# The recurrence's projection: order of its column blocks, and where the bonus product is kept

## The reference

```python
proj = h @ w_in
z, q_mem = proj[..., :RW_SHIFT], proj[..., RW_SHIFT:]
z_prev = jnp.pad(z, ((0, 0), (1, 0), (0, 0)))[:, :-1]
z = z + (z_prev - z) * mu
r, k, v, zw, za, zg = _split(z, [MIX_WIDTH] * 3 + [DECAY_LORA, ICLR_LORA, GATE_LORA])
w_log = -jax.nn.softplus(-(w0 + jnp.tanh(zw) @ w2)) - 0.5
decay = jnp.exp(-jnp.exp(w_log.astype(jnp.float32)))
a = jax.nn.sigmoid(a0 + za @ a2)
g = jax.nn.sigmoid(zg) @ g2
kk = (k * k_k).astype(jnp.float32).reshape(B, S, H, N)
kk = kk / jnp.maximum(jnp.sqrt(jnp.sum(kk * kk, axis=-1, keepdims=True)), 1e-12)
k = k * (1 + (a - 1) * k_a)
...
y = _wkv7_scan(rh, wh, kh, vh, -kk, kk * ah)
...
bonus = jnp.sum(rh * kh * r_k.astype(jnp.float32), axis=-1, keepdims=True) * vh
out = (y + bonus.reshape(B, S, MIX_WIDTH)) * g.astype(jnp.float32)
```

## Time and profile before

| what | us |
|---|---|
| median of 3 runs | 2264.17 (2262.78 to 2269.66) |
| the profiled execution, its own time | 2262.99 |
| its span | 2261.1 |
| TensorE busy | 2106.9 (93%) |
| VectorE busy | 1143.5 (51%) |
| ScalarE busy | 826.4 (37%) |
| mean granted TensorE clock | 0.971 |

### The profile page before, as it was taken

The page is one execution under the profiler, slowest core; times in us unless marked ns, Lnnn a source line. Parts: engine busy times, 40 slices in busy tenths (PEclk is TensorE's granted clock), DMA queues, the critical chain, the costliest instruction groups (busy, mean ns, idle before and its releaser), DMA issues.

```text
span 2261.1 us, 36356 instructions
## 1 busy us (share of the span) xinstructions
PE 2106.9 (93%) x15617; PEld 1141.8 (51%) x15617; DVE 1143.5 (51%) x1755; ACT 826.4 (37%) x1344; POOL 274.1 (12%) x342
## 2 busy tenths in 40 slices
PE   6898889999999998799999999998998888999998
PEld 3566554444444343688744444553565435444444
DVE  4865763444432368665545455234637455655221
ACT  4324763232322664332243234323335334332222
POOL 2311331000001010222210000102012113000000
PEclk9998999999999999999999999998999999999999
DMA  6442002433222312000033433241320021323220
GB/s 147 118 142 67 2 1 70 116 95 107 89 96 84 93 54 75 21 22 4 3 93 95 112 93 103 93 140 57 112 75 20 19 75 38 112 93 110 95 93 38
DMA packets 203844, 173.61 MB, mean 77 GB/s; under 512 B 20416, under 2 KB 179332, under 8 KB 203684
## 3 DMA queue, kind: packets, MB, share of 16 engines
q1 hardware_dynamic: 202778, 170.34, 24.9%
q10 hardware_dynamic: 906, 0.96, 0.2%
HBM read 169.18 MB, written 2.10 MB: 76 GB/s over the span
## 4 chain that ended last, share of the span: by engine, by line
PE 79%; DVE 10%; ACT 6%; issue 3%; POOL 1%; ACTq 0%; DMA 0%; DVEq 0%; POOLq 0%
PE banks L1119 46%; PE banks L1162 17%; PE banks L1410 4%; PE banks L1200 1%; DVE w_lo L2227 1%; ACT w_hi L1679 1%; PE banks L1422 1%; POOL arena L969 1%; ACT arena L1784 1%; PE banks L1220 1%; PE banks L1599 1%; PE banks L1177 1%; PE banks L1522 1%; DVE banks L2325 1%; ACT arena L2069 1%
## 5 line engine op out<-in xcount | busy, mean ns | idle before, releaser
L1119 PE MATMUL banks<-arena,w_hi 128*128 128x512 f16 (+1 forms) x2160 | 628.7, 375 | 5.5 <-DVE arena L2247 3.3
L2227 DVE TENSOR_TENSOR w_lo<-wring,w_hi 128x2048 bf16<-128x2048 f32 (+3 forms) x162 | 357.2, 2206 | 473.8 <-ACT w_hi L1679 470.1
L1679 ACT ACTIVATE w_hi<-wring 128x2048 f16<-128x2048 f32 (+3 forms) x162 | 294.9, 1822 | 462.3 <-PE banks L1162 266.1
L1119 PE MATMUL banks<-arena,w_lo 128*128 128x512 f16 (+1 forms) x1080 | 404.4, 374 | 0.0
L1162 PE MATMUL banks<-arena,w_hi 128*128 128x512 f16 x1216 | 363.2, 381 | 10.9 <-DVE xT L2304 4.4
L1119 PEld LDWEIGHTS banks<-arena,w_hi 128*128 128x128 f16 x2160 | 211.2, 98 | 251.8 <-DVE arena L2247 5.7
L1119 PE MATMUL banks<-h_hi,w_hi 128*128 128x512 f16 (+1 forms) x624 | 239.7, 384 | 18.7 <-DVE w_lo L2227 9.6
L969 POOL TENSOR_TENSOR arena<-arena,ntmp 128x512 f32<-128x512 f32 (+1 forms) x79 | 100.9, 1278 | 1262.6 <-ACT ntmp L1709 1257.1
L1119 PE MATMUL banks<-h_lo,w_hi 128*128 128x512 bf16 (+1 forms) x624 | 239.3, 384 | 0.0
L1119 PE MATMUL banks<-h_hi,w_lo 128*128 128x512 f16 (+1 forms) x624 | 238.9, 383 | 0.0
L1162 PE MATMUL banks<-arena,w_lo 128*128 128x512 f16 x608 | 231.3, 380 | 0.0
(11 more groups left out here) (392 smaller groups left out, 2687.9 us busy)
## 6 DMA issues: line engine op xcount, KB each, us to landing
wring<-in_w_ffn_in SPq DMA_DIRECT2D x88, 512.0 KB, 5.0
wring<-in_w_ff SPq DMA_DIRECT2D x32, 1024.0 KB, 5.1
wring<-in_w_ffn_out SPq DMA_DIRECT2D x20, 1024.0 KB, 5.1
wring<-in_rw_w_in SPq DMA_DIRECT2D x11, 1024.0 KB, 5.2
wring<-in_w_in SPq DMA_DIRECT2D x11, 1024.0 KB, 5.2
wring<-in_nsa_w_in SPq DMA_DIRECT2D x7, 1024.0 KB, 5.3
wring<-in_w_mem_kv SPq DMA_DIRECT2D x4, 1024.0 KB, 5.1
wring<-in_w_o SPq DMA_DIRECT2D x4, 1024.0 KB, 5.1
```

What stands on the lines that cost most here:

```text
L1119: last = mm(v, p[0], p[1], start=(i == 0), stop=(i == len(prods) - 1))
L1679: A(w_hi[:, at[0] % NSPLIT, 0:w["size"]], wring[:, w["slot"], 0:w["size"]], ACT.Copy).then_inc(split_hi, 1)
L2227: V.tensor_tensor(w_lo[:, sl, 0:w["size"]], wring[:, w["slot"], 0:w["size"]], w_hi[:, sl, 0:w["size"]], ALU.subtract).then_inc(split_lo, 1)
```

## The change

```diff
--- before.py
+++ after.py
@@ -657,8 +657,8 @@
             rw_jobs.append((t, mm, dst, v, j, m))
 
         LORA0, ATT0 = 4, 5
-        RP0 = (7, 9, 12, 14, 17, 18)
-        BON0 = (12, 13, 18, 19, 22, 23)
+        RP0 = (7, 9, 12, 14, 16, 18)
+        BON0 = (18, 19, 20, 21, 22, 23)
         rp_tiles = [{} for _ in range(JP)]
 
         def rw_tiles(i):
@@ -681,7 +681,7 @@
             t, mm, v = feature_tile(w, c * P, P, hT, "v")
             rw_jobs.append((t, mm, qm1[:, c, :], v, None, HD ** -0.5))
         rw_tiles(LORA0)
-        for b in (3, 0, 4, 6, 1, 5, 7, 2, 8):
+        for b in (3, 0, 4, 1, 5, 2, 6, 7, 8):
             w = rw_panel(b)
             for c in range(2):
                 shift_job(w, c, 2 * b + c)
@@ -1376,7 +1376,7 @@
             def rp_bonus(j):
                 t = rp_tiles[j]["b"]
                 pe.wait_ge(rp_rk, j + 1)
-                products(t, [(bank[t.bank][:], [(blockones[:], tmp[j][2], None)])])
+                products(t, [(bank[t.bank][:], [(blockones[:], bonT[:, j, :], None)])])
 
             def rw_pieces(i):
                 if 0 <= i - LORA0 < JP:
@@ -2592,7 +2592,8 @@
                 link(V.tensor_scalar(t2_, t1_, -1.0, col("rw_k_a", j), ALU.add, ALU.mult))
                 V.tensor_tensor(t1_, kkT[:, j, :], t1_, ALU.mult)
                 link(V.scalar_tensor_tensor(kT7[:, j, :], t2_, 1.0, kT7[:, j, :], ALU.add, ALU.mult))
-                V.scalar_tensor_tensor(t4_, rT[:, j, :], col("rw_r_k", j), kT7[:, j, :], ALU.mult, ALU.mult).then_inc(rp_rk, 1)
+                dve.wait_ge(rp_exp, j + 1)
+                V.scalar_tensor_tensor(bonT[:, j, :], rT[:, j, :], col("rw_r_k", j), kT7[:, j, :], ALU.mult, ALU.mult).then_inc(rp_rk, 1)
 
             def rp_rest(j):
                 t2_, t3_, t4_, t5_, t6_ = tmp[j]
```

## The result

The changed kernel takes 2276.85 us in the median of six runs (2275.71 to 2279.55); the kernel before, run beside it, 2264.57 us. The ratio is 1.0051 with a 95% interval of 1.0038 to 1.0063: half a per cent slower. 1.0051 times the median that the prediction started from, 2264.17, is 2275.7; the raw median, 2276.85, lies 0.35 above the top of the range. The profiled execution took 2276.14 us, its span is 2274.4 us.

A forecast was written before the change was run, and what follows sets the result against it. TensorE bounds the whole kernel, but VectorE was taken to end the changed stage; its holes, -3.00 + 2.00 + 0.61 + 4.68 + 4.07 = +8.36 us, gave 2271.4 to 2272.5, stated as 2272.0, range 2263.5 to 2276.5.

The forecast's parts named there:

- (a): Slot 12: VectorE no longer waits for the bonus of pair 0, -3.00 us.
- (b): Product 14: VectorE comes too early and waits for TensorE, +2.00 us.
- (c): Slot 16: squares of pair 4 come before ScalarE's high half and lengthen the existing hole, +0.61 us.
- (d): Slot 18: VectorE has too little work while ScalarE makes factors and squares before the high half, +4.68 us.
- (e): Slot 20: keys and rest of pair 4 have left, so VectorE waits for ScalarE's high half, +4.07 us.
- (f): The added wait for rp_exp before the bonus product costs nothing; uncovered, some 0.7 us a pair.
- (g): TensorE's pauses move, about 6 us before the norms of pairs 4 and 5, longer before the last bonus, and stay cover.
- the high sum: All unknown terms of the stage taken high: +10.45 us.
- sum of low terms: All unknown terms of the stage taken low: -1.92 us.
- Rival 1: Slots 19 and 21: high halves are ready in time, no holes open; -0.39 us, 2263.8, not slower; chance 0.12.
- rival 2: TensorE sets the stage's pace, its 6.82 us pause and the 3.00 us go: 2254.4, faster; chance 0.07.
- Rival 3: Slots 17 to 23: TensorE's slow clock after three pauses reaches VectorE, 5.40 us more: 2277.9; chance 0.09.

The follow-up runs named there:

- e1: The changed kernel with one table entry, RP0[4], set back from 16 to 17: 2264.82 us, ratio to before 1.001.
- e2: The kernel before with only the bonus product's place changed (to bonT) and the added waits for rp_exp: 2263.52 us, ratio 0.9994.
- f3: The kernel before with only the bonus products late (slots 18 to 23) and in bonT, old panel order and RP0: 2265.61 us, ratio 1.0002.
- e3: The changed kernel with ScalarE's high half issued ahead of the pieces in even slots from slot 6: 2263.64 us, ratio to before 0.9994.
- f2: The kernel before with twelve linked maxima added on VectorE ahead of its last two bonus products: 2278.94 us, ratio 1.0058.
- f4: e3 with RP0 = (7, 9, 11, 14, 15, 17), keys of pairs 2, 4 and 5 one slot earlier: 2257.53 us, ratio to before 0.9970.
- h3: The changed kernel with only RP0 = (7, 9, 11, 14, 15, 17), high half where it stood: 2258.64 us, ratio to before 0.9971.
- e4: The kernel before with ScalarE's high half issued ahead of the pieces in even slots from slot 6: 2263.43 us, ratio 0.9995.
- h4: The kernel before with six linked maxima added on VectorE ahead of its last two bonus products: 2273.02 us, ratio 1.0032.

## Why the prediction was right

The direction, the mechanism and its place were right. The size was not: 12.3 us in the medians where 7.8 were forecast; by the ratio that is 0.8 us inside the upper end of the range. Step by step, measured against forecast:

| step | forecast | measured |
|---|---|---|
| (a) bonus of pair 0 out of slot 12 | -3.00 | -3.00 |
| its side: the wait for L1173, 0.22 before | not in the sum | +0.52 (0.74) |
| (b) wait for product 14 | +2.00 | +1.50 |
| (c) squares 4 in front of the high half | +0.61 | +0.61 (5.28) |
| (d) hole of slot 18 | +4.68 | +4.55 |
| (e) hole of slot 20 | +4.07 | +3.95 |
| stage | +8.36 | +8.13 by these, +8.14 by the rows |
| outside the stage | 0 | 4.2 (medians) to 5.2 (first profile) |

- (a) to (e) need no correction of kind. The way from read to low half in slot 18 is 901.66 - 895.04 = 6.62, forecast 6.61. Most of the 0.12 that (d) and (e) are short, 0.09, is the bonus, whose end no next instruction overlaps: it takes 0.69, its duration, where I had taken the 0.60 from start to start.
- (b) and the 0.52 belong together. I had reckoned with the slow clock behind the 3.11 us pause at product 13, but not that it would slow the four passes just behind the pause, on which VectorE waits: 1.23 us in place of 0.70. In e1, where they took 0.70, the wait for product 14 was 2.10, so the two together are 2.02 and 2.10: the forecast's 2.00 was right for the pair. The 0.52 is not of the change's making: the wait is 0.74 in e2 and f3 too, which have the old order, and 0.21 in e1 and e3, which have the new one.
- (f) is shown right by e2: the added wait costs nothing and no row shows it.
- (g) was half right: the pauses moved and stayed cover, but the second is 4.24 us, not "about 6", and the last, 4.91, is not longer than these.
- The range's bounds were not all worked out: 2274.6 is 2264.2 plus the high sum, but no sum of low terms gives 2268.5.
- Rival 1 (holes don't open) and rival 2 (TensorE sets the pace) are refuted by the four holes, and rival 2 also by f2, where a delay of VectorE went through one to one. A little further on rival 2 gains ground: in f4 and h3 it is TensorE that VectorE waits for.
- On the busiest engine, the section of the Trainium skill that the prediction quotes ("Perfetto Trace Analysis", Identifying the Most-Contended Engine) sets TensorE apart: it wants it judged by weight loads or by its share of peak arithmetic, not by busy matmuls. By weight loads TensorE has 19.29 us of the 45 and VectorE 30.32, so read in full the rule points at VectorE here, as the trace does.
- Rival 3 named the right cost in the wrong place. Slow matmuls did cost what is missing, but not on VectorE's way in the stage: the stage is shorter than forecast. That its 2277.9 lies nearer to the median than 2272.0 does is therefore luck.

**The step that failed** is the scope of the sum, which took the rest of the program as unchanged: "nothing behind takes that back", and no term for what it might add. I wrote that I would be wrong if the time differed outside 800 to 930 us, and a third of it did: 4.0 us ahead and 1.2 behind in the profile, 12.3 - 8.1 = 4.2 us in the medians. What the runs put in its place: TensorE pauses of 2 to 3 us at fixed places, in code that no edit touches, are followed by slow stretches whose length differs from kernel to kernel and, as far as the times tell, from execution to execution. What decides their length stays open. Of the 4.0 us ahead only 1.69 lies at such a place that I can show; 1.0 is there by 32 us and 2.5 by 121, in the first, much interrupted part of the program, and I did not trace these further. Nor do I know why the change shows them in three profiles of three while e1, which differs from it by one table entry much later in the program, came 0.82 late. One thing the fourteen profiles show: seven are 1.7 us or more late by 750 us (the change's three, e2, e3, e4 and f3), and just these have the longer slow stretch near 766; the other seven are at most 1.6 late there and don't. So what is late in the first part and that stretch come together, whatever the kernel's edit. Profiles of both a short and a long execution of one kernel would be the next thing to take.

Profiles taken once would have misled: e3's was 5.1 us above its median, and e4's showed a stage gain of 4.16 of which the median kept 1.2.

## What to carry to other kernels

In a hand-ordered pipeline ask of every slot what stands ahead of the instruction that the other engine waits for, and what that engine has of its own to do meanwhile: moving one pair's steps by one slot opened holes of 8.5 us here, and moving three pairs' so that the work falls into the holes made the kernel 0.3% faster than before. An edit that changes nothing by itself, here the order of the panels, can be what makes such a move possible. Such a sum, made from a few rows, can be right to 0.3 us for the stage; for the whole program leave a margin: what came outside the stage, slow stretches behind TensorE's pauses among it, was half as much again here. And judge an edit of this size by its stage in the trace first, and by the median of many executions second, never by one execution's total.

## What was unexpected of the hardware

The same pause doesn't bring the same slow stretch. Behind the 3.13 us pause in front of L1162 the matmuls ran at once at full clock, 2.4 GHz, in both profiles of before and in those of e1, e2, f2, f3 and h3; they ran at 1.2 GHz long enough to cost 1.5 us in the change's three, in e4 and in f4, and 2.9 us in e3 and h4. The granted clock over the 12 us from the pause's end takes three values to match: 1.00, 0.87 and 0.75. Behind the 2.30 us pause of slot 4 it is 0.86, 0.72 or 0.57. The times of one kernel step with the mean granted clock: h3's twelve executions took 2255.9 to 2257.3 us at 0.974 (six of them), 2260.0 to 2261.0 at 0.972 (four), and 2261.7 and 2265.8 at 0.971. Of the 76 executions of before beside the experiments, 60 have 0.971 and a median of 2264.1 us, ten have 0.970 or less and 2266.0 to 2272.8. All 17 of the change have 0.967 to 0.969.

The Trainium skill ("TensorE: Matmul & The Clock Gate", Part 1) says that the number of slow matmuls varies from run to run of the same kernel, since what watches the activity doesn't start with the kernel. The times of h3, and those of e3 (2259.5 to 2268.8 us, at 0.972 down to 0.969), agree with that, as far as a mean clock tells it. The change's three profiles, 1.20, 1.14 and 1.14 us behind the stage, and its 17 executions without one at a higher clock, are steadier than that sentence would have them.
